# Weight slots over memory freed by the output projection, the router inside it, and scatters that add gated expert rows into a second copy of h1

## The reference, cut to what matters

```python
h1 = layer_norm(DN_ALPHA * x + cat @ w_o, ln1_g, ln1_b)
# top-1 of 4 groups (p_group), top-2 of its 8 experts (w2 = softmax over the two)
gate = p_group * w2            # zero for the 30 other experts
f = sum over experts e of (silu(h1 @ w_gate[e]) * (h1 @ w_up[e]) * gate[e]) @ w_down[e]
y = layer_norm(DN_ALPHA * h1 + f, ln2_g, ln2_b)
```

## Time and profile before

| | |
|---|---|
| median of 3 runs | 992.29 us |
| the profiled execution | 994.26 us, its span 992.4 us |
| granted TensorE clock, mean over the span | 0.953 |
| busy | PE 902.3 us (91%), DVE 578.0 (58%), ACT 387.9 (39%), POOL 186.9 (19%) |
| DMA | 273.51 MB, mean 276 GB/s; weights and plain copies on q1, indirect rows on q0 |
| chain that ended last | PE 82%, DVE 10%, ACT 3%, DMA 3%, issue 2% |

### The profile page before, as it was taken

One profiled execution on the slowest core, in us unless ns is written; L12 is line 12 of the kernel. 1 busy time (PEld: TensorE's weight loads), 2 busy tenths in 40 slices (PEclk: granted clock), 3 DMA queues, 4 the chain that ended last, 5 costly groups with the idle time before them and its releaser, 6 DMA issues.

```text
span 992.4 us, 13499 instructions
## 1 busy us (share of the span) xinstructions
PE 902.3 (91%) x5178; PEld 649.0 (65%) x5178; DVE 578.0 (58%) x1178; ACT 387.9 (39%) x739; POOL 186.9 (19%) x85
## 2 busy tenths in 40 slices
PE   6999999987899999868999985999999999999944
PEld 6999879963555545536888864666666666666521
DVE  6202020038665665684687775578787878787438
ACT  5202020024455645472111022464646464645136
POOL 0000000050000000000000003155555555555200
PEclk9999999998999999997999975999999999999967
DMA  9999999299776857507742069899999999997285
GB/s 355 305 351 362 369 344 344 90 359 265 255 290 241 298 168 245 203 24 261 254 170 85 27 233 332 304 348 366 361 353 361 348 360 371 364 371 270 84 313 221
DMA packets 54850, 273.51 MB, mean 276 GB/s; under 512 B 13985, under 2 KB 16545, under 8 KB 39681
## 3 DMA queue, kind: packets, MB, share of 16 engines
q1 hardware_dynamic: 46016, 247.97, 69.7%
q0 software_dynamic: 8768, 24.66, 7.1%
HBM read 256.33 MB, written 95.30 MB: 354 GB/s over the span
## 4 chain that ended last, share of the span: by engine, by line
PE 82%; DVE 10%; ACT 3%; DMA 3%; issue 2%; SPq 0%; DVEq 0%; POOLq 0%; ACTq 0%
PE psum L667 75%; PE psum L726 4%; PE psum L939 2%; DVE back L1276 1%; DMA back<-h_d,back 1%; ACT back L510 1%; DVE back L1258 1%; DMA middle<-pair_d 1%; DVE stats L1261 1%; PE psum L865 1%; ACT back L1049 1%; DVE front L1284 1%; DVE front L1286 1%; PE psum L962 1%; DVE back L510 0%
## 5 line engine op out<-in xcount | busy, mean ns | idle before, releaser
L1699 POOL DMA_INDIRECT pair_d<-front,back x32 | 134.7, 4208 | 167.7 <-DVE front L1540 167.7
L667 PE MATMUL psum<-back,front 128*64 128x128 f32 (+1 forms) x904 | 151.6, 360 | 5.3 <-ACT back L510 4.4
L667 PEld LDWEIGHTS psum<-back,front 128*64 128x64 f32 (+1 forms) x904 | 71.3, 148 | 61.0 <-issue 52.4
L667 PE MATMUL psum<-gu_high,xg_high 128*112 128x512 f32 x256 | 103.9, 406 | 0.9 <-DVE xg_low L1525 0.9
L667 PE MATMUL psum<-gu_high,xg_low 128*112 128x512 f32 x256 | 101.9, 398 | 0.0
L667 PE MATMUL psum<-x_high,w_high 128*128 128x352 f32 x288 | 93.9, 326 | 8.3 <-DVE w_low L376 8.3
L667 PE MATMUL psum<-gu_low,xg_high 128*112 128x512 f32 x256 | 101.1, 395 | 0.0
L667 PE MATMUL psum<-x_low,w_high 128*128 128x352 f32 x288 | 93.2, 324 | 0.0
L667 PE MATMUL psum<-x_high,w_low 128*128 128x352 f32 x288 | 93.1, 323 | 0.0
L667 PE MATMUL psum<-front 64*128 64x256 f32 (+5 forms) x320 | 79.8, 521 | 10.8 <-DVE stats L1258 10.5
L1540 DVE SCALAR_TENSOR_TENSOR front<-psum,back 112x512 f32<-112x512 f32 x64 | 45.1, 747 | 68.8 <-PE psum L667 68.8
(11 more groups left out here) (209 smaller groups left out, 1682.8 us busy)
## 6 DMA issues: line engine op xcount, KB each, us to landing
back<-w_gu SPq DMA_DIRECT2D x32, 1024.0 KB, 15.9
out_win_k_s<-cache_win_k SPq DMA_DIRECT2D x16, 2044.0 KB, 13.7
out_win_v_s<-cache_win_v SPq DMA_DIRECT2D x16, 2044.0 KB, 12.3
back<-w_down SPq DMA_DIRECT2D x25, 1024.0 KB, 15.1
front<-w_gu SPq DMA_DIRECT2D x16, 1024.0 KB, 13.2
middle<-w_gu SPq DMA_DIRECT2D x16, 1024.0 KB, 13.9
back<-winkT SPq DMA_DIRECT2D x8, 1792.0 KB, 7.3
back<-cache_win_v SPq DMA_DIRECT2D x8, 1024.0 KB, 7.5
```

The lines of the kernel that those rows point to most:

```text
L667: return nc.tensor.matmul(out, lhsT, rhs, start=start, stop=stop, skip_group_check=True)
L1699: G.indirect_dma_start(pair_d, bass.IndirectOffsetOnAxis(ap=IDX[0:CAP, NE + e:NE + e + 1], axis=0), YS[e % 2][0:CAP, :], None, bounds_chec ...
```

## The change

- **Memory map.** The rounded and rest parts of cat are laid out block by block, the rest part moves to the place of x's projection scratch (35472), and the slots of the expert weights (`GU_AT`, `GUH_AT`, `WD`) move over memory that the output projection frees as it goes. The experts' small tiles move to the start of `front`, over w_o's rounded part.
- **Loads.** SP issues w_gu of experts 0 to 2 and w_down of expert 0 inside the output projection (after its blocks 3, 4 and 5 and on), not after it.
- **Mixer.** The pool differences, the sample queries and the rests of w_o go from DVE to POOL, behind the sums. In the cross units one minimum and one reciprocal serve both heads; their score tiles stand 512 words apart.
- **Output projection.** cat's high and low parts of blocks 0 to 3 are made up front, the others four blocks ahead. Each `mix` is cut in the first three and the last five of its eight parts, and `rank` and `router` stand between the pieces. On DVE `chosen(c-1)` stands ahead of `first_norm(c)`, `placed(c-1)` behind it. The last block's turn also makes slot 0 of the weights ready.
- **Gates** go ahead of expert 0's transposes on PE.
- **Experts.** They are taken by turns over the four groups (`TURN`: 0, 8, 16, 24, 1, ...). `y_out` is gate x product only, and the scatter adds it (`compute_op=ADD`) to the token's row in `sum_d`, which each block's second store of h1 has filled. The first scatter waits for all these stores.
- **Tail.** One row per token is fetched, and the sums over pairs on PE and DVE are gone. Two small activations load ACT's tables ahead of their use.

The diff, cut to its core:

```diff
+TURN = [(n % NG) * EPG + n // NG for n in range(NE)]
...
-        CATH, CATL = overlay("cat_high", 8448, KT, TOK), overlay("cat_low", 18576, KT, TOK)
-        GU_AT, GUH_AT = (0, 18576, 27024, 37520), (4096, 22672)
+        CATH, CATL = overlay("cat_high", 8448, 1, KT * TOK)[:, 0], overlay("cat_low", 35472, 1, KT * TOK)[:, 0]
+        GU_AT, GUH_AT = (8448, 18576, 37520, 27024), (22672, 4096)
...
-        WD = [at(x, 2, D) for x in (11264, 44688, 46736, 48784, 41616)]
+        WD = [at(x, 2, D) for x in (12544, 41616, 44688, 46736, 48784)]
...
             def store_h1(c):
                 sp.wait_ge(s_h1, c + 1)
                 sp.dma_start(h1_d[c * P:c * P + rows(c), :], H1[0:rows(c), c, :]).then_inc(s_h1d, 16)
+                sp.dma_start(sum_d[c * P:c * P + rows(c), :], H1[0:rows(c), c, :]).then_inc(s_init, 16)
...
+                if c == 5:
+                    sp.wait_ge(s_mix, 4)
+                    for half in range(2):
+                        load_gu(sp, 0, half)
+                if c == 6:
+                    sp.wait_ge(s_lo, len(splits) + CH)
+                    for half in range(2):
+                        load_gu(sp, 1, half)
+                if c == 7:
+                    sp.wait_ge(s_mix, 6)
+                    load_dn(sp, 0)
+            for half in range(2):
+                load_gu(sp, 2, half)
+            store_h1(CH - 2)
             sp.wait_ge(s_mix, CH)
             for half in range(2):
-                load_gu(sp, 0, half)
-            for c in range(CH - 2, CH):
-                store_h1(c)
-            load_dn(sp, 0)
-            for e in (1, 2):
-                for half in range(2):
-                    load_gu(sp, e, half)
-                load_dn(sp, e)
-            sp.wait_ge(s_ht, 2 * CH)
+                load_gu(sp, 3, half)
+            store_h1(CH - 1)
+            load_dn(sp, 2)
+            load_dn(sp, 3)
+            sp.wait_ge(s_ht, 2 * (CH - 1))
             sp.wait_ge(s_h1d, 16 * CH)
-            for half in range(2):
-                load_gu(sp, 3, half)
+            sp.wait_ge(s_init, 16 * CH)
+            load_dn(sp, 1)
+            sp.wait_ge(s_gs, 1)
...
-                sp.dma_start(YP[c][0:rows(c), :, :], pr[c * P:c * P + rows(c), :, :]).then_inc(s_yp[c], 16)
+                sp.dma_start(RF[c][0:rows(c), :], sum_d[c * P:c * P + rows(c), :]).then_inc(s_sum2[c], 16)
...
-            def mix(c, n):
-                if n == 0 and c >= 2:
+            def mix(c, n, ks):
...
+                    if c == 0 and n == 0:
+                        pe.wait_ge(s_wol, k + 1)
...
+            first, second = range(0, 3), range(3, KT)
             for c in range(CH):
-                mix(c, 0)
+                mix(c, 0, first)
+                if c >= 2:
+                    rank(c - 2)
+                mix(c, 0, second)
                 if c:
                     h1_transposes(c - 1)
-                mix(c, 1)
+                mix(c, 1, first)
                 if c:
                     router(c - 1)
-                if c >= 2:
-                    rank(c - 2)
+                mix(c, 1, second)
+            rank(CH - 2)
...
-            pe.wait_ge(s_idx, 1)
+            gates()
             gather_transposes(0)
-            gates()
...
-                    o = row_sum(c)[0:m, 512 * n:512 * n + 512]
-                    mm(o, ident[0:m, 0:m], YP[c][0:m, 0, 512 * n:512 * n + 512], True, False)
-                    last = mm(o, ident[0:m, 0:m], YP[c][0:m, 1, 512 * n:512 * n + 512], False, True)
...
+            for c in range(CH):
+                m = rows(c)
+                if c >= 1:
+                    h1t_copy(c - 1)
+                if c == CH - 1:
+                    act.wait_ge(s_lo, len(splits) + CH)
+                    weights_rounded(0)
+                act.wait_ge(s_mv, c + 1)
+                nc.scalar.activation(MV[0:m, c, 2:3], MV[0:m, c, 1:2], ACT.Sqrt, bias=EPSC[0:m, :]).then_inc(s_std, 1)
+                if c + 4 < CH:
+                    cat_rounded(c + 4)
+            h1t_copy(CH - 1)
...
-                    V_.tensor_reduce(MN[:, x:x + 1], ps[:, 0:N_MEM], AX.X, ALU.min).then_inc(s_min, 1)
+                elif s:
+                    dve.wait_ge(s_S, x + 1)
+                    both = PS[:, score_at(u, 0):score_at(u, 0) + 1024].rearrange("p (a n) -> p a n", a=2)[:, :, 0:N_MEM]
+                    V_.tensor_reduce(MN[:, x - 1:x + 1], both, AX.X, ALU.min).then_inc(s_min, 2)
...
+                if kind == "c" and s == 0:
+                    return
+                first = x if kind == "w" else x - 1
                 dve.wait_ge(s_exp, x + 1)
-                V_.reciprocal(RD[:, x:x + 1], DEN[:, x:x + 1]).then_inc(s_rd, 1)
+                V_.reciprocal(RD[:, first:x + 1], DEN[:, first:x + 1]).then_inc(s_rd, x + 1 - first)
                 dve.wait_ge(s_rd, x + 1)
-                V_.tensor_scalar(p, p, RD[:, x:x + 1], None, ALU.mult).then_inc(s_norm, 1)
+                for y in range(first, x + 1):
+                    p = SP[(u % 3) * 2 + y % 2][:, 0:w]
+                    V_.tensor_scalar(p, p, RD[:, y:y + 1], None, ALU.mult).then_inc(s_norm, 1)
...
-                if u == 2:
-                    sample_queries()
-                if u == 3:
-                    pool_differences(0)
-                if u == 4:
-                    pool_differences(1)
                 for e in extra[u]:
                     x_out(e)
-                for k in WO_SPLIT_AT.get(u, ()):
-                    full, high, low = wo_parts(k)
-                    dve.wait_ge(s_hi, len(splits) + k + 1)
-                    V_.tensor_tensor(low, full, high.bitcast(F32), ALU.subtract).then_inc(s_lo, 1)
...
+                if c:
+                    chosen(c - 1)
                 first_norm(c)
-                if c + 2 < CH:
-                    cat_rest(c + 2)
-                if c >= 1:
-                    chosen(c - 1)
-                if c >= 2:
-                    placed(c - 2)
+                if c + 4 < CH:
+                    cat_rest(c + 4)
+                if c:
+                    placed(c - 1)
+                if c == CH - 2:
+                    weights_rest(0, (0, 1))
+            weights_rest(0, (2, 3))
...
-                    V_.scalar_tensor_tensor(YS[e % 2][0:CAP, h], bank(4 + n)[0:CAP, :], GS[0:CAP, e:e + 1], XG[e % 5][0:CAP, h],
-                                            ALU.mult, ALU.add).then_inc(s_yd, 1)
+                    V_.tensor_scalar(YS[e % 2][0:CAP, h], bank(4 + n)[0:CAP, :], GS[0:CAP, TURN[e]:TURN[e] + 1], None,
+                                     ALU.mult).then_inc(s_yd, 1)
...
+            for t in range(2):
+                for g in range(2):
+                    r = slice(64 * g, 64 * g + 64)
+                    src = (PA, PBUF)[g]
+                    step(G.tensor_tensor(PA[r, t, UH:UH + 16], src[r, t, UH:UH + 16], pool_inv[r, t, 0:16], ALU.mult))
+                    step(G.tensor_tensor(PA[r, t, UH:UH + 16], PA[r, t, UH:UH + 16], UP[r, t, UH:UH + 16], ALU.subtract))
+                    step(G.tensor_scalar(PA[r, t, UH + 16:UH + SEQ], src[r, t, UH + 16:UH + SEQ], pool_inv[r, t, 16:17], None, ALU.mult))
+                    step(G.tensor_tensor(PA[r, t, UH + 16:UH + SEQ], PA[r, t, UH + 16:UH + SEQ], UP[r, t, UH + 16:UH + SEQ], ALU.subtract))
...
+            for k in range(KT):
+                full, high, low = wo_parts(k)
+                pool.wait_ge(s_hi, len(splits) + k + 1)
+                G.tensor_tensor(low, full, high.bitcast(F32), ALU.subtract).then_inc(s_wol, 1)
+                pool.wait_ge(s_wol, k + 1)
...
-                G.indirect_dma_start(pair_d, bass.IndirectOffsetOnAxis(ap=IDX[0:CAP, NE + e:NE + e + 1], axis=0), YS[e % 2][0:CAP, :], None,
-                                     bounds_check=last_pair, oob_is_err=False).then_inc(s_ys[e % 2], 16)
+                G.indirect_dma_start(sum_d, bass.IndirectOffsetOnAxis(ap=IDX[0:CAP, TURN[e]:TURN[e] + 1], axis=0), YS[e % 2][0:CAP, :], None,
+                                     bounds_check=last_token, oob_is_err=False, compute_op=ALU.add).then_inc(s_ys[e % 2], 16)
```

256 lines of the change are left out of this document (99 added, 157 removed).

## The result

The changed kernel takes 1002.17 us (median of 6 runs, 1000.19 to 1004.93), the kernel before 994.15 us (6 runs, 992.18 to 996.69). The ratio is 1.0087, 95% interval 1.007 to 1.0104: 0.9% slower. The forecast was 985 us with a range of 962 to 1008: the measured time lies inside the range, but it is a loss where a gain was forecast. The profiled execution of the changed kernel has a span of 998.2 us against 992.4, so the two traces hold 5.8 of the 8.0 us between the medians. (Matmuls that were line 667 are now line 665; later lines differ a little from run to run.)

What follows compares the result with a forecast made beforehand. PE was taken to bound most of the span, with DMA lag in the experts nearly used up. Terms -6 - 4 + 3.5 - 9 + 20 - 12 = -7.5 from the 992.4 us span gave 985 us, range 962 to 1008.

Steps and rivals of the forecast that it cites:

- part 1: Front of the mixer: moving the memset, sample-query copies and pool differences from DVE to POOL, -6 us (bounds -11 and +4).
- Part 2: Cross attention: w_o rests leave DVE and one reduction serves both heads, -4 us (bounds -9 and +5).
- rival D: Mixer ports: POOL's passes hold up DVE, front and cross attention give +4 and +5, kernel 1004 us; chance 0.08.
- Part 3: Output projection: with the new order PE waits 0.5 us for h1 in seven blocks, +3.5 us (bounds 0 and +5).
- Part 4: Last block to first expert: first gate_up at +31.2 against +39.9 us, taken as -9 (bounds -6 and -11).
- Part 5: Experts: the adding scatter costs the busiest DMA engines 0.96 us per expert, +20 us after 6.5 us of slack.
- Rival A: Experts: the add is hidden, under 0.7 us per expert; expert term 0, kernel 965 us; chance 0.25.
- rival C: Experts: the adding scatter costs more than two transfers, 1.7 us per expert, term +40.6, kernel 1005 us; chance 0.15.
- Part 6: Tail: one fetch per token and no sums over pairs, end at 980.6 us, -12 us (bounds -9 and -13).
- Faster: Whole kernel: faster by more than the 0.5% (5 us) that a measurement can tell from no change; chance 0.55.

## Why the prediction was wrong, step by step

Forecast and trace, by the same marks:

| part | forecast us | trace us | how read |
|---|---|---|---|
| 1, 2: mixer | -10 | -3.5 | first matmul 454.33 to 450.86 |
| 3: output projection | +3.5 | +5.7 | end of the last matmul 579.24 - 454.33 = 124.9 against 581.42 - 450.86 = 130.6 |
| 4: to expert 0 | -9 | -9.2 | 39.9 against 30.7 |
| 5: experts | +20 | +22.4 | first product to last silu, 314.6 against 337.0 |
| 6: tail | -12 | -9.6 | last silu to end, 58.7 against 49.1 |
| sum | -7.5 | +5.8 | spans 992.4 to 998.2 |

- **Parts 1 and 2 are the step that failed**, by 6.5 of the 13.3 us. The prediction had the mechanism, as rival D with a chance of 0.08, and its arithmetic (ten divisions with half a pass each, 9 us): measured are 13.8 us for 14 divisions in place of 6.8, so 7 us. But it kept -6 for part 1, a larger gain than the middle of its bounds (-3.5). It set against D that DVE is free for 12 of 52 us in the cross stage; that time was no argument, since PE waits for a held division at once (PE waited for divisions 14.8 us in the mixer, 13.0 before, although DVE was busy 151.2 us up to the first matmul and not 163.8). The move of part 1 brought about 4 us. Part 2's -4 was about nothing: the move of w_o's rests +0.6 us, and what is left of the mixer's 3.5, the one reduction for both heads included, is within the 2 us of a mark (that reduction was not tried by itself). POOL's passes are 2.35 us, not the 1.9 of the earlier trace rows; the next pass of the same sums, over 128x1025 elements (L1664), took 2.36 in the trace before.
- **Part 3**: the wait of 0.5 us for h1 came out as 0.41 in seven blocks, as predicted:

```profile
484.03 1.09 PE L865 MATMUL psum<-consts,back 128*128 128x128 f32 x8 [0.41 <-DVE back L1369]
```

  A block takes 14.84 us in place of 14.19. Beside that wait the new order costs another 0.2 us a block, which the prediction had at nothing; with the old order the block is back at 14.21. Whether it is the cutting in pieces or the place of router and rank was not tried.
- **Part 4** was right in size. (The parts given for IDX add up to +16.3, not +16.9; the sum goes on from 16.9.) The last block is taken up by DVE at 582.44, 1.0 us after PE's end, because chosen stands ahead, as worked out.
- **Part 5** was right in its size and in its mechanism: a lag of those engines alone that carry rows, and the point at which the slots are used up. Between the run without the add and the changed kernel the last load of w_gu lands at 910.3 us (issued at 888.3) and at 936.9, where ACT's timeline in the changed kernel ends a wait for it:

```profile
936.88 2.00 ACT L1109 CAST gu_high<-back 128x1024 fp32r<-128x1024 f32 x2 [0.43 <-DMA back<-w_gu]
```

  26.6 us over 27.7 loads are 0.96 us per expert, where 0.96 was taken (in part luck: it was taken as the middle between two prices, not worked out). The landing grew faster than that up to 740 us, by 1.7 us per expert more than without the add, and less after, since rows reach the engines at PE's pace and not at the loads'. The 6.5 us that were to be hidden were about 5, as the stage grew by 21.8. Rival A fell, and so did C: its 1.7 us per expert is the early growth of the landing and not the price of the add.
- **Part 6** missed 2.4 us: 2.0 of it is the adding scatter's landing, 5.58 for 3.61 us, which stood in the bound of -9 as 3 and in the sum as nothing. The first block's fetch (3.53) was as taken.

The Trainium skill (Collectives: The Full Stack, section on the bandwidth ceiling and fold count) led to 1.21 us for the add; measured are 0.96 in the mean by the landings. Its factor of two for an add fits the packets: the queue's time per MB goes from 45 to 64 us with half of its bytes added, so an added row takes about 84 us per MB, 1.85 times a written one (an estimate), and the add of 28.7 KB costs 1.1 us. That this is a second read no trace shows. The Trainium skill (SBUF — State Buffer, section on its two separate sides) spoke of an exclusive lock for a whole instruction: the division of 2.32 us that ends with POOL's pass agrees, for POOL's two-input passes. Beside the one-input pass the trace does not agree: a division began and ended inside it at its length of 0.35 us.

"Faster" at 0.55 rested on parts 1, 2 and 6 being gains of 22 us; they were 13.1. With the mixer at its -10 the sum would have been -0.7: parts 3, 5 and 6 each missed by 2.2 to 2.4 us, all to the slow side. That the measured 1002 lies near the 1004 of rival D and the 1005 of rival C is chance: D had +9 for the mixer, which gained 3.5, and C had 1.7 us for the add, which cost 0.96.

## What to carry to other kernels

Ask not only how many bytes an indirect transfer moves but on which DMA engines its rows lie: a list filled from the front of the partitions loads some engines more than others, and permuting the list cost nothing here (993.46 us against 993.72). Work moved to POOL can come back as longer instructions on DVE: two-input passes did so here, beside divisions and beside a subtraction, copies did not. A landing time that grows from issue to issue is a debt that no wait shows until the slots are used up: price every addition against what is left of it.

## What the runs showed of the hardware beyond that

- The last scatter, with no load beside it, takes 1.97 us longer adding than writing (5.58 against 3.61), and 1.8 us longer with the rows spread (4.70 against 2.90).
- The indirect queue's packets (gathers and scatters) took 44 to 48 us per MB with writing scatters (three kernels) and 63 to 66 with adding ones (five kernels), from 640 to 740 us and from 760 to 900 us alike; with every second scatter adding, 54.
- POOL's two-input pass held a DVE division for up to 2.0 us and a DVE subtraction of two operands for 1.1; beside its one-input pass of 2.8 us divisions took between 0 and 0.44 us more, beside its copies none.
- POOL's pass with one input and a constant (64 x 1008) took 2.8 us, longer than its two-input pass with 2.30 to 2.43.
